# Hybrid flow-matching step: minima and exponentials of score chunks taken one or two PSUM banks at a time

## What is computed

```
def block_attention(q, k, v, mix):              # swept over 128-query blocks
    s = einsum('bqhgcd,bkhcd->bhgcqk', q, k * d ** -0.5)
    p = einsum('bhgcqk,c->bhgqk', softmax(s, axis=-1), mix)
    return einsum('bhgqk,bkhe->bqhge', p, v)

# layer 0: 4 heads, two softmax maps a head, mix = (1, -lambda), d = 64, values 128 wide
# layer 1: 16 query heads in 4 groups (one key/value head each), mix = (1,), d = 64
# a context query sees the 128 context keys; a latent query sees 1024 latent + 128 cached keys
```

## Time and profile before

| | us |
|---|---|
| median of three runs | 3990.02 (3986.44 to 3990.7) |
| span of the profiled execution | 3988.1 |
| differential attention, first to last score minimum | 890.0 to 1181.5 |
| grouped-query attention, first to last score minimum | 2448.0 to 2973.6 |

### The profile page before, as it was taken

How to read it: one execution, slowest core, us unless ns; L and a number is a source line. 1 busy time by engine, 2 the same in 40 slices (tenths; PEclk the granted TensorE clock), 3 DMA queues, 4 the chain that set the end, 5 groups by cost and what they waited for, 6 DMA issues and landing times. The chain is left out here.

```text
span 3988.1 us, 52620 instructions
## 1 busy us (share of the span) xinstructions
PE 3424.4 (86%) x17646; PEld 2961.2 (74%) x17646; DVE 1966.0 (49%) x3464; ACT 1161.0 (29%) x2474; POOL 1820.2 (46%) x1700
## 2 busy tenths in 40 slices
PE   7789993647768799999999686888888799999998
PEld 2377873536666699999998574777777699999998
DVE  7764115677772433333333675888883433333333
ACT  5611001146650310110110313888870310110110
POOL 0053102536551245545545354888871245545545
PEclk9899996859998899999999796999999899999999
DMA  8612212020002111110110212000002110110111
GB/s 331 253 69 98 87 45 77 5 94 17 15 7 90 50 44 34 53 42 32 53 42 1 103 61 78 17 16 16 18 1 90 53 43 32 53 42 32 53 42 48
DMA packets 118990, 232.74 MB, mean 58 GB/s; under 512 B 64064, under 2 KB 71360, under 8 KB 108736
## 3 DMA queue, kind: packets, MB, share of 16 engines
q1 hardware_dynamic: 118880, 231.33, 17.0%
HBM read 197.74 MB, written 34.34 MB: 58 GB/s over the span
## 5 line engine op out<-in xcount | busy, mean ns | idle before, releaser
L812 POOL TENSOR_TENSOR x<-x,ff_gated 128x512 f32<-128x512 f32 x396 | 512.1, 1293 | 320.1 <-DVE ff_gated L897 296.6
L806 POOL TENSOR_TENSOR ff_lo<-ff_raw,ff_hi 128x1024 fp32r<-128x1024 f32 x132 | 329.0, 2499 | 547.2 <-ACT ff_hi L773 547.0
L897 DVE TENSOR_TENSOR ff_gated<-ff_y_banks,gate_tokens 128x512 f32<-128x512 f32 x396 | 273.8, 691 | 412.6 <-PE ff_y_banks L871 411.2
L610 PE MATMUL tile_sum<-w_hi,tokens_hi 128*128 128x512 f32 x1008 | 405.1, 402 | 68.5 <-DVE w_lo L641 45.0
L773 ACT ACTIVATE ff_hi<-ff_raw 128x1024 fp32r<-128x1024 f32 x132 | 137.9, 1061 | 1118.7 <-PE ff_y_banks L871 720.5
L886 DVE TENSOR_TENSOR ff_silu<-ff_silu,ff_up_banks 128x384 f32<-128x384 f32 x132 | 72.5, 550 | 718.2 <-PE ff_up_banks L842 718.2
L611 PE MATMUL tile_sum<-w_lo,tokens_hi 128*128 128x512 f32 x1008 | 403.0, 400 | 0.0
L612 PE MATMUL tile_sum<-w_hi,tokens_lo 128*128 128x512 f32 x1008 | 402.3, 399 | 0.0
L838 PE MATMUL ff_gate_banks<-tokens_hi,ff_hi 128*128 128x384 f32 x1056 | 354.6, 336 | 19.4 <-POOL ff_lo L806 19.4
L839 PE MATMUL ff_gate_banks<-tokens_lo,ff_hi 128*128 128x384 f32 x1056 | 354.1, 335 | 0.0
L839 PE MATMUL ff_up_banks<-tokens_lo,ff_hi 128*128 128x384 f32 x1056 | 353.2, 334 | 0.0
(11 more groups left out here) (254 smaller groups left out, 7481.8 us busy)
## 6 DMA issues: line engine op xcount, KB each, us to landing
ff_raw<-in_w_ffn SPq DMA_DIRECT2D x132, 512.0 KB, 3.5
mod_raw<-in_w_mod SPq DMA_DIRECT2D x48, 1024.0 KB, 6.9
scratch_mixer_in<-tile_out SPq DMA_DIRECT2D x90, 256.0 KB, 2.0
w_raw<-in_w_in_even SPq DMA_DIRECT2D x14, 1024.0 KB, 6.4
q_double<-scratch_mixer_in SPq DMA_DIRECT2D x72, 128.0 KB, 2.3
w_raw<-in_w_in_odd SPq DMA_DIRECT2D x6, 1024.0 KB, 6.6
x<-in_x SPq DMA_DIRECT2D x9, 512.0 KB, 7.4
q_double<-scratch_mixer_in SPq DMA_DIRECT2D x72, 64.0 KB, 2.0
```

The lines of the kernel that those rows point to most:

```text
L610: nc.tensor.matmul(acc, self.hi[:, k, mine], w_hi, start=(k == 0), stop=False)
L806: pool.tensor_tensor(lo[:, u], raw[:, slot], hi[:, u].bitcast(F32), ALU.subtract).then_inc(lo_done, 1)
L812: pool.tensor_tensor(self.x[:, t, cols], self.x[:, t, cols], y[:, m % YB], ALU.add).then_inc(added, 1)
```

## The change

The three chunks of a latent map are in banks b, b+1 and b+2 modulo 4. Two whose banks are neighbours without a wrap are now taken by one instruction. So a map has two **parts**: where its first chunk is in bank 3 the parts are one chunk and two chunks, otherwise two and one. The minimum reduces over both axes of a 128x2x384 operand, and the exponential writes 768 columns and gives one row sum. Layer 1 has parts two-one, one-two, two-one, two-one for its maps 0 to 3. Layer 0 has two-one, one-two for an even head and two-one, two-one for an odd one.

All counts follow: `e_done` and `reduced` rise by two a map, POOL adds two sums and not three, and PE's wait before chunk n is for the part that holds chunk n - 4. The order of PE's instructions stays. What DVE does between the first and second chunk minimum is now between the first and second part.

```diff
+def bank_parts(chunks, bank):
+    if chunks == 1:
+        return [(0, 1)]
+    return [(0, 1), (1, 2)] if bank == 3 else [(0, 2), (2, 1)]
+
+def part_of(chunks, bank, chunk):
+    return next(i for i, (a, n) in enumerate(bank_parts(chunks, bank)) if a <= chunk < a + n)
...
+            def freed(self, n, after_ctx):
+                back = n - 4
+                if back < 0 and (self.ctx or after_ctx):
+                    return self.e + (n - 3)
+                m, c = back % 12 // 3, back % 3
+                return self.e + (2 * m + part_of(3, 3 * m % 4, c) + 1 - (8 if back < 0 else 0))
...
                             pool.tensor_tensor(sum_, parts[:, 0:1], parts[:, 1:2], ALU.add).then_inc(summed, 1)
-                            pool.wait_ge(summed, x.sums + (3 * m + 1))
-                            pool.tensor_tensor(sum_, sum_, parts[:, 2:3], ALU.add).then_inc(summed, 1)
-                            pool.wait_ge(summed, x.sums + (3 * m + 2))
+                            pool.wait_ge(summed, x.e + (2 * m + 1))
...
-                            pe.wait_ge(e_done, x.s + (n - 3))
+                            pe.wait_ge(e_done, x.freed(n, isinstance(x.t, int) and x.t == 1 and x.g == 0))
...
-                        for c in range(x.chunks):
+                        for i, (c, cnt) in enumerate(bank_parts(x.chunks, x.head_bank(m))):
                             if m == 0 and w is not None:
-                                act.wait_ge(pt_turned, w.tr + (1 if w.ctx else 3 * c + 3))
-                            nc.scalar.activation(probs[:, x.slot, m, c * x.width:(c + 1) * x.width],
-                                                 sbank[:, (m * x.chunks + c) % 4, 0:x.width], ACT.Exp,
+                                act.wait_ge(pt_turned, w.tr + (1 if w.ctx else 3 * (c + cnt)))
+                            bank = (x.head_bank(m) + c) % 4
+                            nc.scalar.activation(probs[:, x.slot, m, c * x.width:(c + cnt) * x.width].rearrange("p (c k) -> p c k", c=cnt),
+                                                 sbank[:, bank:bank + cnt, 0:x.width], ACT.Exp,
...
-                        for c in range(ch):
-                            n = m * ch + c
-                            dve.wait_ge(s_done, x.s + (n + 1))
-                            nc.vector.tensor_reduce(low[:, i, c:c + 1], sbank[:, n % 4, 0:x.width], AX.X, ALU.min).then_inc(reduced, 1)
-                            if c == 0 and between is not None:
+                        for j, (c, cnt) in enumerate(bank_parts(x.chunks, x.head_bank(m))):
+                            bank = (x.head_bank(m) + c) % 4
+                            dve.wait_ge(s_done, x.s + (m * x.chunks + c + cnt))
+                            nc.vector.tensor_reduce(low[:, i, j:j + 1], sbank[:, bank:bank + cnt, 0:x.width], AX.XY, ALU.min).then_inc(reduced, 1)
+                            if j == 0 and between is not None:
                                 between()
```

More of the change, by code:

```diff
@@ L1032, in __init__ @@
                 self.s = self.n * 2 if ctx else (t - 1) * (6 * M) + (2 * M + 6 * h)
+                self.parts = 1 if ctx else 2
+                self.e = self.n * 2 if ctx else (t - 1) * (4 * M) + (2 * M + 4 * h)
                 self.bank = (2 * h if ctx else 6 * h) % 4
@@ L1036, in __init__, with map_bank @@
                 self.slot = h % 2
+            def map_bank(self, m):
+                return (self.bank + m * self.chunks) % 4
+            def freed(self, n, after_ctx):
+                back = n - 4
+                if back < 0 and (self.ctx or after_ctx):
+                    return self.e + (n - 3)
+                if back < 0:
+                    before = (self.bank - 6) % 4
+                    m, c = (back + 6) // 3, (back + 6) % 3
+                    return self.e + (2 * m + part_of(3, (before + 3 * m) % 4, c) + 1 - 4)
+                m, c = back // 3, back % 3
+                return self.e + (2 * m + part_of(3, self.map_bank(m), c) + 1)
         def step_units(t, h, kind):
@@ L1119, in row_sum @@
                         sum_, parts = total[:, x.slot, m:m + 1], sums[:, x.slot, m]
-                        pool.wait_ge(e_done, x.s + x.chunks * (m + 1))
+                        pool.wait_ge(e_done, x.e + x.parts * (m + 1))
                         if x.ctx:
@@ L1176, in scores @@
                         if not (x.ctx and x.h < 2):
-                            pe.wait_ge(e_done, x.s + (n - 3))
+                            pe.wait_ge(e_done, x.freed(n, isinstance(x.t, int) and x.t == 1 and x.h == 0))
                         m, c = n // x.chunks, n % x.chunks
@@ L1319, in maximum @@
                     def maximum(x, m, v, w):
-                        ch = x.chunks
-                        for c in range(ch):
-                            n = m * ch + c
-                            dve.wait_ge(s_done, x.s + (n + 1))
-                            nc.vector.tensor_reduce(low[:, m, c:c + 1], sbank[:, (x.bank + n) % 4, 0:x.width], AX.X, ALU.min).then_inc(reduced, 1)
-                            if m == 0 and c == 0:
+                        for i, (c, cnt) in enumerate(bank_parts(x.chunks, x.map_bank(m))):
+                            bank = (x.map_bank(m) + c) % 4
+                            dve.wait_ge(s_done, x.s + (m * x.chunks + c + cnt))
+                            nc.vector.tensor_reduce(low[:, m, i:i + 1], sbank[:, bank:bank + cnt, 0:x.width], AX.XY, ALU.min).then_inc(reduced, 1)
+                            if m == 0 and i == 0:
                                 probs_lo(w, 0)
-                        dve.wait_ge(reduced, x.s + (m + 1) * ch)
+                        dve.wait_ge(reduced, x.e + (m + 1) * x.parts)
                         if v is not None:
-                            dve.wait_ge(e_done, x.s - v.chunks * (1 - m))
-                        nc.vector.tensor_reduce(nb[:, m:m + 1], low[:, m, 0:ch], AX.X, ALU.min).then_inc(m_done, 1)
+                            dve.wait_ge(e_done, x.e - v.parts * (1 - m))
+                        nc.vector.tensor_reduce(nb[:, m:m + 1], low[:, m, 0:x.parts], AX.X, ALU.min).then_inc(m_done, 1)
                     def mix(v):
@@ L1421, in __init__, with head_bank, freed @@
                 self.ring = g if ctx else M + NB * g
-                self.sums = self.n * M if ctx else (t - 1) * (3 * M * M) + (M * M + 3 * M * g)
+                self.parts = 1 if ctx else 2
+                self.e = self.n * M if ctx else (t - 1) * (2 * M * M) + (M * M + 2 * M * g)
                 self.slot = g % 2
+            def head_bank(self, m):
+                return m * self.chunks % 4
+            def freed(self, n, after_ctx):
+                back = n - 4
+                if back < 0 and (self.ctx or after_ctx):
+                    return self.e + (n - 3)
+                m, c = back % 12 // 3, back % 3
+                return self.e + (2 * m + part_of(3, 3 * m % 4, c) + 1 - (8 if back < 0 else 0))
         def step_units(t, g, kind):
```

46 lines of the change are left out of this document (21 added, 25 removed).

## The result

| | before | after |
|---|---|---|
| median of the runs | 3990.36 (4 runs, 3986.44 to 3996.47) | 4064.09 (4 runs, 4058.61 to 4067.73) |
| ratio, with its 95% interval | 1 | 1.0183 (1.017 to 1.0196) |
| span of the profiled execution | 3988.1 | 4065.9 |
| layer 0, first to last score minimum | 890.0 to 1181.5 = 291.5 | 893.0 to 1208.9 = 315.9 (+24.4) |
| layer 1, first to last score minimum | 2448.0 to 2973.6 = 525.6 | 2475.7 to 3051.9 = 576.2 (+50.6) |

The change costs 73.7 us by the medians. 75 of the 77.8 us between the two spans lie in the two attentions; layer 0 also begins 3 us later, within the 889 to 894 us at which it begins in the profiles here.

What follows compares the result with a forecast made beforehand. A circle of waits through PE, ACT and DVE, not a full engine, was taken to pace layer 1; DVE and its waits, layer 0. 3988.1 + 66 (50 layer 1, 16 layer 0) + 1.9 = 4056 us; own range 4035 to 4080, overall 4012 to 4098.

Steps and rivals of the forecast that it cites:

- What bounds: Both attentions: no engine is full; a circle of waits paces them, in layer 1 15.96 us a unit through PE, ACT, DVE.
- The price of a double: Both attentions: two-chunk exponential 0.91 us, ending 0.33 later than the first single (ends 0 and 0.55); two-chunk reduce 0.95 us.
- Layer 1: Step: 1.0 for three longer exponential waits plus 0.6 for DVE's order, 1.6 us a unit; 31 units, 50 us.
- map 3's order: Layer 1, DVE: the double reduce and the pT_lo behind it make map 3's last reduce 0.2 us late.
- The halving of map 1's 0.40: Layer 1: map 1's closing double reduce takes 0.40 us longer; half taken as hidden before qT_lo, leaving 0.2 a unit.
- map 2's own 0.2: Layer 1, DVE: the double waits for chunk 7, then pT_lo follows, so chunk 8's reduce starts 0.2 us late.
- Layer 0: Step: head 0 loses 0.8, head 1 0.75, head 2 0.45, head 3 nothing; 2.0 us a tile, 8 tiles, 16 us.
- only the exponential binds: Rival: DVE's order is hidden; layer 1 loses 1.0 a unit, 31 us, layer 0 8; total 4029; chance 0.15.
- Faster: Rival: engines' own work, ACT's first, paces the loops; gains 31 us in layer 1, 4 in layer 0; 3955; chance 0.08.
- no change: Rival: gain and delay cancel, double exponential releasing its banks as early as a single; within 0.2%, 3990; chance 0.05.
- a double costs as two: Rival: exponential 0.55 late, not 0.33; 20 us more in layer 1, some 5 in layer 0; 4081; 0.12 with the clock.
- The clock: Rival: longer waits lower PE's clock, 1.7 us in every second layer 1 unit, 27 us; 4083; 0.12 shared with doubles as two.

Runs made afterwards that it cites:

- off_circle_chunks: off_circle with one change: e_done and reduced rise by a part's number of chunks, so all counters run at one rate; 3990.88 us, ratio 1.0002.
- layer1_only: The change in layer 1 alone, with layer 0 as before the change; 4040.76 us, ratio 1.0129.
- turn_first: The change with DVE's pT_lo piece (probs_lo in layer 0) moved ahead of a double first reduce, in both attentions; 4043.77 us, ratio 1.0136.
- the fill: The change plus eight unread matmuls of 256 columns ahead of layer 0's third product, where PE idles; 4060.79 us, ratio 1.0181.
- min_only: Against the kernel before: minima in two parts as in the change, exponentials still in three, both attentions; 4025.72 us, ratio 1.0095.
- exp_only: Against the kernel before: exponentials in two parts as in the change, minima still in three, both attentions; 4029.64 us, ratio 1.0105.
- exp_late: exp_only in layer 1 alone, with map 3's exponential as one chunk then two, not two then one; 4016.39 us, ratio 1.0068.
- off_circle: Kernel before, with double exponentials only in layer 1's map 1 (one-two) and layer 0's second map, minima in three; 3995.95 us, ratio 1.0017.

## Why the prediction came out as it did

The forecast was 4056, the result 4064. The mechanism is the one forecast, and one term is missing from the sum, the clock in layer 0. Step by step:

- **What bounds.** Right. The engines' totals fell and the time rose by as much as a circle of waits through PE, ACT and DVE says. off_circle_chunks shows the other side: work taken off ACT and POOL, with the circle left alone, is worth nothing (ratio 1.0002).
- **The price of a double.** 0.91 and 0.95 us by estimate, 0.902 and 0.955 measured. Of the two ends of the range, no delay and 0.55, neither was near; the slope between the 128 and the 384 rows was.
- **Layer 1.** The sum gave 1.6 us a unit and 50 in all; it is 1.54 and 50.6, and layer1_only gives 51.1 in the medians. By legs the sum says: 2 to 3, 0.33 for chunk 10 and 0.2 for map 3's order, 0.53; measured 0.53. 0 to 1, the 0.33 each of chunks 1 and 4 and the 0.40 by which map 1's double ends later, 1.06; measured 1.09. 1 to 2, its own 0.2 less the 0.2 of map 1 that was to be hidden, 0; measured -0.02. The halving of map 1's 0.40, which was a middle between two ends and no more, is seen in turn_first: without map 2's own 0.2 that leg is 0.23 below the one of before, so what is hidden is that much. That the layer fits to 0.6 us is in part luck. 31 units at 1.54 are 47.7; the first unit took 16.1 us for 13.2, 2.9 more and not 1.5. PE's clock was mostly at its lower level there (a window of that unit and one of the steady part, as above):

```profile
2512.00:2527.00 15.00, 11.59 (x40) 0.54 0.08 19
2600.00:2900.00 300.00, 240.63 (x1411) 1.00 0.07 15
```

In the steady part it stayed at 1.00, as argued.
- **Layer 0.** This is the term that was mis-sized: 16 forecast, 24.4 in the profile and 22.6 by the medians. The steps of the sum are right where PE's clock is undisturbed: from the first `minus_max` of head 0 to that of head 1 it is 9.13 us for 7.98 (+1.15; the sum has 0.33 and 0.2 of head 0 and 0.6 of head 1 there, 1.13), 1 to 2 +0.61 (the rest of head 1, 0.15, and 0.45), 2 to 3 -0.13 (none), 3 to 0 +0.43 (0.25), together 2.06 for 2.0, or 16.5 us in eight tiles for the 16 of the sum. The other 8 us are the lower clock in this profile: 10.9 us in tiles 2 to 7 where it took 4.8, which is 6.1, and 1.6 more in the first tile. That a stretch with the same 43 matmuls is 9.13 us at a clock of 1.00 and 10.48 at 0.84 shows it within one execution, and the layer is at +16.0 with the fill. The prediction had this mechanism, but as a rival, and priced it only for layer 1. In layer 0, where PE is less busy and its clock already fell to 0.66 behind a gap, it should have had a place in the sum. For the runs without a kept trace less is shown. The 22.6 us that the medians give layer 0 are 6 more than the sum at a clock of 1.00, which fits a clock lost in those runs too; but the fill brought back no more than 2 to 3 us of it in the medians, inside their scatter.
- **The rivals.** That only the exponential binds falls with min_only, 36 us for the minima alone. Faster, or no change, fall with the result; the faster case rested on ACT's load, and 0.25 us less of ACT a map gave nothing even where it cost nothing. That a double costs as two falls with its 902 ns. The clock came in, for some 8 us, in the layer where it hadn't been priced, and not in every second unit of layer 1, where it had.
- **Signs in the profile.** Score waits of 1.16 us, three a unit where about 1.0 was said; exp_only has 1.11 (87.9 us in 79), so it comes with the exponentials; `pT_lo` directly behind the double and no idle time ahead of the last part, seen; unit 17.5, seen. POOL's wait grew from 1.5 to 3.3 us a unit, by 1.8 where over 2 was said. The layer 0 tile was to be 35 and is 39.0 on the mean, with 35.9 before: the window of 33 us that I had taken for a tile was shorter than one.

The Trainium skill, page VectorE: DVE Perf Modes, section The TRN2 errata, says of operands in SBUF that their latency lies between instructions and that one large tile pays it once. The operands here are read from PSUM, and the work shows the same: a map's two exponentials are 0.25 us shorter than its three (902 and 577 ns for 3 x 581; in the timelines 1.46 us for 1.71 from first start to last end). That says nothing on when the first result comes, and here that decided.

## What to carry to other kernels

Merging instructions saves their fixed cost, and delays whatever hangs on the first of them: here 0.25 us saved a map on an engine with time to spare, against 0.33 us three times a unit on the path. So mark, before merging, which piece releases a buffer that the next engine stands before, and merge only the others (exp_late got 0.24 us a unit back for the one it moved); when a first piece becomes larger, also move what was queued behind it to ahead of it, which gave back 0.4 us a unit here. And where the merged engines aren't the bound, expect nothing even from a merge that costs nothing.

## What the runs showed of the hardware

- One ACTIVATE and one TENSOR_REDUCE over two PSUM banks (128x768 of 2 x 384 columns) cost by columns alone: 902 and 955 ns, as the line through 128 and 384 columns gives (estimated 0.91 and 0.95). Having the second half of the operand in the next bank costs nothing that can be seen.
- A register computation ahead of a wait lies on DVE's path between two dependent instructions: 0.68 us instead of 0.60 from the last reduce to `minus_max`. Two semaphores that rise at different rates in a hardware loop cost 5 to 6 us in off_circle, and nothing once they rise at one rate (off_circle_chunks); in exp_only the same mending gave 0.05 us a unit and nothing in the median. It isn't shown as busy time, only as more distance between two starts.
- PE's granted clock in the profiled layer 0 fell more often with PE's added waits: 0.97 before, 0.92 after, and 0.98 with eight unread matmuls in one of the idle stretches of each unit. The same 43 matmuls took 9.13 us from head 0 to head 1 at a clock of 1.00 and 10.48 at 0.84. The profiled layer got 8.4 us shorter with the added matmuls, the median of the runs 3.3; with off_circle_chunks as the base it was 2.2 us in the profile and nothing in the median.

Open: why exp_only's unit is 0.1 us longer than three times 0.33 even with the counters mended, and how much of layer 0's 8 us the clock takes in the executions of which no trace was kept.
